# Recurrent layer of a two-layer trunk: gelu of the gate branch as one ScalarE function read from PSUM, and the square of the decay and the first tap of the convolution moved from VectorE to ScalarE

## The reference, cut to what matters

```python
def rglru(x, h0, ga_w, ga_b, gx_w, gx_b, lam):
    r = jax.nn.sigmoid(block_diag(x, ga_w, ga_b).astype(jnp.float32))
    i = jax.nn.sigmoid(block_diag(x, gx_w, gx_b).astype(jnp.float32))
    log_a = -RG_C * r * jax.nn.softplus(-lam.astype(jnp.float32))
    a = jnp.exp(log_a)
    mult = jnp.sqrt(-jnp.expm1(2.0 * log_a))
    bterm = mult * (i * x.astype(jnp.float32))
...
def rglru_mixer(x, conv_buf, h0, w_in, conv_w, conv_b, ga_w, ga_b, gx_w, gx_b, lam, w_out):
    gx = jnp.einsum('bsd,de->bse', x, w_in)
    gate, xr = jnp.split(gx, 2, axis=-1)
    xc, new_buf = causal_dwconv(xr, conv_buf, conv_w)
    xc = xc + conv_b
    h, h_last = rglru(xc, h0, ga_w, ga_b, gx_w, gx_b, lam)
    y = jnp.einsum('bsc,cd->bsd', jax.nn.gelu(gate, approximate=True) * h, w_out)
```

## Time and profile before

| | |
|---|---|
| median of 3 runs | 1391.53 us (1390.49 to 1392.58) |
| span of the profiled execution | 1387.8 us |
| PE, PEld busy | 96%, 64% of the span |
| DVE, ACT, POOL busy | 543.0, 217.6, 122.2 us |
| recurrent mixer on PE | from 704.7 us to about 887 us |
| mean granted TensorE clock | 0.997 of full speed |

### The profile page before, as it was taken

How to read it: one execution, slowest core, us unless ns; L and a number is a source line. 1 busy time by engine, 2 the same in 40 slices (tenths; PEclk the granted TensorE clock), 3 DMA queues, 4 the chain that set the end, 5 groups by cost and what they waited for, 6 DMA issues and landing times.

```text
span 1387.8 us, 20245 instructions
## 1 busy us (share of the span) xinstructions
PE 1337.2 (96%) x8652; PEld 891.7 (64%) x8652; DVE 543.0 (39%) x1157; ACT 217.6 (16%) x383; POOL 122.2 (9%) x138
## 2 busy tenths in 40 slices
PE   8999999999999999998899999999999999999896
PEld 7888875656555555664488888666555555556552
DVE  5677766331111211241446878642211111223217
ACT  0000114000000000100134453310000001010012
POOL 0000001111000110121010000010001100111100
PEclk9999999999999999999999999999999999999999
DMA  9700469999999999999992113899999999999995
GB/s 390 296 5 1 172 278 356 407 426 425 426 427 426 427 424 427 424 425 425 373 327 100 61 61 122 303 380 428 424 427 427 424 427 425 426 426 424 425 404 218
DMA packets 67874, 472.48 MB, mean 340 GB/s; under 512 B 16414, under 2 KB 26654, under 8 KB 40127
## 3 DMA queue, kind: packets, MB, share of 16 engines
q1 hardware_dynamic: 51773, 449.37, 78.1%
q0 software_dynamic: 11520, 15.52, 3.2%
q10 hardware_dynamic: 4490, 6.27, 1.5%
HBM read 468.38 MB, written 27.32 MB: 357 GB/s over the span
## 4 chain that ended last, share of the span: by engine, by line
PE 85%; DMA 10%; ACT 2%; DVE 2%; issue 1%; POOL 0%; POOLq 0%; SPq 0%; DVEq 0%
PE ps L1086 28%; PE ps L1122 14%; PE ps L778 10%; PE ps L732 9%; PE ps L822 7%; PE ps L1051 7%; DMA ring<-in_moe_w_down 3%; DMA ring<-in_moe_w_up 3%; PE ps L1039 3%; PE ps L1110 1%; PE ps L1062 1%; PE ps L839 1%; DMA ring<-yrows 1%; DMA yrows<-A,Bt 1%; PE ps L1224 1%
## 5 line engine op out<-in xcount | busy, mean ns | idle before, releaser
L1086 PE MATMUL ps<-ring,A 128*64 128x256 f32 x4096 | 457.7, 380 | 14.5 <-DMA ring<-in_moe_w_up 6.5
L1086 PEld LDWEIGHTS ps<-ring,A 128*64 128x64 f32 x4096 | 327.4, 137 | 155.1 <-issue 40.0
L1122 PE MATMUL ps<-ring,A 128*64 128x512 f32 x1024 | 233.8, 597 | 7.0 <-issue 1.1
L2026 DVE TENSOR_TENSOR A<-A,ps 128x256 f32<-128x256 f32 x64 | 27.0, 421 | 540.5 <-PE ps L1086 540.5
L1122 PEld LDWEIGHTS ps<-ring,A 128*64 128x64 f32 x1024 | 75.9, 136 | 119.4 <-issue 113.5
L732 PE MATMUL ps<-A,ring 128*128 128x260 f32 x576 | 129.4, 386 | 0.9 <-DMA ring<-in_a_w_in 0.9
L732 PEld LDWEIGHTS ps<-A,ring 128*128 128x128 f32 x576 | 110.5, 192 | 18.5 <-DMA ring<-in_a_w_in 1.2
L667 POOL DMA_INDIRECT A<-x,idx x42 | 44.5, 1060 | 671.9 <-PE ps L1039 623.9
L1051 PE MATMUL ps<-C,Bt 104*64 104x512 f32 x400 | 95.6, 620 | 0.0
L2029 DVE COPY A<-ps 128x256 f32<-128x256 f32 x64 | 27.2, 425 | 121.0 <-PE ps L1110 121.0
L1439 ACT ACTIVATE A<-ps 128x512 f32<-128x512 f32 x42 | 25.1, 598 | 306.1 <-PE ps L1122 306.1
(11 more groups left out here) (295 smaller groups left out, 1137.3 us busy)
## 6 DMA issues: line engine op xcount, KB each, us to landing
ring<-in_moe_w_gate SPq DMA_DIRECT2D x62, 2048.0 KB, 20.3
ring<-in_moe_w_up SPq DMA_DIRECT2D x60, 2048.0 KB, 23.2
ring<-in_moe_w_down SPq DMA_DIRECT2D x60, 2048.0 KB, 29.1
ring<-yrows SPq DMA_DIRECT2D x10, 1024.0 KB, 9.6
ring<-in_a_w_in SPq DMA_DIRECT2D x6, 1536.0 KB
ring<-in_moe_w_down SPq DMA_DIRECT2D x8, 1024.0 KB, 44.1
ring<-in_b_w_in SPq DMA_DIRECT2D x8, 1024.0 KB, 12.0
ring<-in_moe_w_up SPq DMA_DIRECT2D x6, 1024.0 KB, 43.6
```

Of the source, the lines that this page charges most:

```text
L1086: mm = pe.matmul(ps[hf * ROWS:(hf + 1) * ROWS, (GATE_BANK, 3)[u], :FH], xgT[:, k, :], ring[:, slot, col:col + FH], start=(k == 0), stop=(k ...
L1122: mm = pe.matmul(ps[nh * ROWS:(nh + 1) * ROWS, 2, :], hidT[:, at:at + ROWS], ring[:, slot, m * D + nh * 512:m * D + (nh + 1) * 512], start ...
L2026: tt(gated, gated, ps[:, 3, :FH], ALU.mult).then_inc(ready, 1)
```

## The change

The Tanh approximation of the gelu was built of a Copy and a Tanh on ACT and four DVE operations. Now the copy of banks 2 and 3 on ACT is itself the function `Gelu_apprx_tanh`, and `gate_cube`, the Tanh of line 1314 and the DVE operation of line 1735 are gone. The square of the decay moves from DVE (1732) to ACT as `Square`, behind the second Tanh and ahead of the Sqrt. The first tap of the convolution, with its bias, moves from DVE (`tsc` on line 1509, called in `conv`) to ACT as an `Identity` with scale and bias, right behind the copy to `pad`. DVE's last product of a chunk loses its factor 0.5.

```diff
                     act.wait_ge(lam_ok, 3)
                     for c in range(KT):
...
                         act.activation(pad[:, WB - 1:].rearrange("p (a b) -> p a b", a=2), banks(0),
                                        ACT.Copy).then_inc(ev_a[1], 1)
+                        act.wait_ge(ev_a[1], c + 1)
+                        act.activation(tmp[8][:, :SEQ], pad[:, :SEQ], ACT.Identity, bias=feat[:, c, R_BB:R_BB + 1],
+                                       scale=feat[:, c, R_WB:R_WB + 1]).then_inc(tap_in, 1)
                         act.wait_ge(mm_in[1], 2 * c + 2)
                         if c >= 2:
                             act.wait_ge(h_done[1], c - 1)
-                        act.activation(halves(tmp[c % 2]), banks(1), ACT.Copy).then_inc(ev_b[1], 1)
+                        act.activation(halves(tmp[c % 2]), banks(1), ACT.Gelu_apprx_tanh).then_inc(ev_b[1], 1)
                         if c >= 1:
                             recurrence_gates(c - 1)
-                    gelu(KT - 1)
                     early_copies(0, 4)
                     recurrence_gates(KT - 1)
@@ recurrence_gates
-                        if c < KT - 1:
-                            gelu(c)
+                        act.wait_ge(act_gate, 4 * c + 2)
+                        act.activation(tmp[2], tmp[4], ACT.Square).then_inc(act_gate, 1)
                         act.wait_ge(sq_in, c + 1)
-                        act.activation(tmp[2], tmp[2], ACT.Sqrt, scale=0.25).then_inc(act_gate, 1)
+                        act.activation(tmp[2], tmp[2], ACT.Sqrt, scale=-0.25).then_inc(act_gate, 1)
@@ conv, on DVE
-                        step(tsc(G1[:, :SEQ], pad[:, :SEQ], tap(R_WB, c), ALU.mult, tap(R_BB, c), ALU.add))
+                        dve.wait_ge(tap_in, c + 1)
@@ recurrence, on DVE
-                        if c < KT - 1:
-                            gate_cube(c)
                         dve.wait_ge(sig_ok, 2 * c + 2)
                         step(stt(I, I, 1.0, x, ALU.add, ALU.mult))
-                        if c == KT - 2:
-                            gate_cube(KT - 1)
-
-                        dve.wait_ge(act_gate, 4 * c + (2 if c < KT - 1 else 3))
-                        step(stt(R, DEC_A, -1.0, DEC_A, ALU.mult, ALU.mult))
-                        stt(R, R, -1.0, TH, ALU.add, ALU.mult).then_inc(sq_in, 1)
                         dve.wait_ge(act_gate, 4 * c + 3)
-                        step(stt(G, G, 1.0, g, ALU.add, ALU.mult))
+                        stt(R, R, 1.0, TH, ALU.add, ALU.mult).then_inc(sq_in, 1)
...
-                        stt(hT[:, c, :], G, 0.5, TH, ALU.mult, ALU.mult).then_inc(h_done[1], 1)
+                        dve.wait_ge(ev_b[1], c + 1)
+                        tt(hT[:, c, :], g, TH, ALU.mult).then_inc(h_done[1], 1)
```

More of the change, by code:

```diff
@@ L26 @@
 RG_C = 8.0
-GELU_C = 0.7978845608028654
-GELU_A = 0.044715
 GROUPS = 4
@@ L243, in build @@
         pad = C[:, 9 * T:10 * T + WB - 1]
-        def g1_tile(c):
-            return tmp[8] if c < KT - 1 else pad[:, :T]
         xk = [C[:TT, i * D:(i + 1) * D] for i in range(NT)]
@@ L388, in build @@
         act_gate = sem("act_gate")
-        gelu_in = sem("gelu_in")
+        tap_in = sem("tap_in")
         piece_ok = sem("piece_ok")
@@ L1311, in _ @@
                 if l == 1:
-                    def gelu(c):
-                        act.wait_ge(gelu_in, c + 1)
-                        act.activation(g1_tile(c), g1_tile(c), ACT.Tanh, scale=GELU_C).then_inc(act_gate, 1)
                     def recurrence_gates(c):
@@ L1691, in _ @@
                 if l == 1:
-                    R, I, DEC_A, TH, G1 = tmp[2], tmp[3], tmp[4], tmp[5], tmp[8]
+                    R, I, DEC_A, TH, FIRST_TAP = tmp[2], tmp[3], tmp[4], tmp[5], tmp[8]
                     dve.wait_ge(xn_done, 2 * NT)
@@ L1699, in conv @@
                         x = tmp[6 + c % 2]
-                        dve.wait_ge(ev_a[1], c + 1)
+                        out = FIRST_TAP
                         if c >= 2:
                             dve.wait_ge(h_done[1], c - 1)
+                        dve.wait_ge(ev_a[1], c + 1)
                         dve.tensor_copy(new_cols[:, c, :11], pad[:, SEQ:SEQ + 11])
-                        step(tsc(G1[:, :SEQ], pad[:, :SEQ], tap(R_WB, c), ALU.mult, tap(R_BB, c), ALU.add))
-                        step(stt(G1[:, :SEQ], pad[:, 1:SEQ + 1], tap(R_WB + 1, c), G1[:, :SEQ], ALU.mult, ALU.add))
@@ L1706, in conv @@
-                        dve.tensor_copy(G1[:, SEQ:], conv0[:, 1, c, :])
-                        step(stt(G1[:, :SEQ], pad[:, 2:SEQ + 2], tap(R_WB + 2, c), G1[:, :SEQ], ALU.mult, ALU.add))
-                        stt(x, pad[:, WB - 1:], tap(R_WB + 3, c), G1, ALU.mult, ALU.add).then_inc(xc_done, 1)
-                        dve.wait_ge(xc_done, c + 1)
[L1711 to L1718, removed]
+                        dve.tensor_copy(out[:, SEQ:], conv0[:, 1, c, :])
@@ L1720, in recurrence @@
+                        dve.wait_ge(tap_in, c + 1)
+                        step(stt(out[:, :SEQ], pad[:, 1:SEQ + 1], tap(R_WB + 1, c), out[:, :SEQ], ALU.mult, ALU.add))
+                        step(stt(out[:, :SEQ], pad[:, 2:SEQ + 2], tap(R_WB + 2, c), out[:, :SEQ], ALU.mult, ALU.add))
+                        stt(x, pad[:, WB - 1:], tap(R_WB + 3, c), out, ALU.mult, ALU.add).then_inc(xc_done, 1)
+                        dve.wait_ge(xc_done, c + 1)
                     def recurrence(c):
-                        x, g, G = tmp[6 + c % 2], tmp[c % 2], g1_tile(c)
+                        x, g = tmp[6 + c % 2], tmp[c % 2]
```

## The result

| | before | changed |
|---|---|---|
| median of 12 runs each | 1389.7 us | 1392.55 us |
| lowest and highest | 1387.92, 1392.58 us | 1390.15, 1396.64 us |
| span of the profiled execution | 1387.8 us | 1391.3 us |
| DVE, ACT busy | 543.0, 217.6 us | 513.6, 234.4 us |

The ratio is 1.0021 with a 95% interval of 1.0012 to 1.0031: 2.9 us more, from 1.7 to 4.3. This is small, but it stands clear of no difference. The 12 runs of the kernel before that stand beside the changed one have a lower median than the three that the prediction had, by 1.8 us.

A forecast was written before the change was run, and what follows sets the result against it. PE was taken to bound the mixer. Chunk 7's delay, 0.03 + 1.28 + 0.65 - 0.27 = 1.69 us, less 0.21 of room leaves 1.48; 1391.5 + 1.5 = 1393.0 us, range 1390.9 to 1394.6.

The forecast's parts named there:

- The bound, and the cover of DVE's work: In the mixer PE is full, 148.00 of 148.00 us, so taking under 34 us off DVE counts as nothing.
- The middle, cost nothing: In each mid-mixer chunk ACT's Sqrt ends about 0.67 us later, covered by PE's product, so the cost is nothing.
- were ACT over 8.8 us later in each chunk, PE would stop: Claimed limit of ACT's room in the middle of the mixer, 8.8 us in each chunk.
- rival 3: Slower, PE stopping mid-mixer: 1.0 us past ACT's 8.8 us room gives 1397.5 and more, 1399.0 with the end; 3%.
- The end: At the mixer's end a load behind ACT's wait and the Square delay chunk 7's Sqrt 1.69 us, router weights 1.48.
- the two stops: PE idles about 0.4 us near 849.7 at the late products, and 1 us more before the router's first matmuls.
- What becomes of it: Behind the mixer the 1.48 us delay stays in full, with no DMA backlog to absorb it.
- The whole tail moves as one piece: Behind the mixer, experts limited by transfers that begin only then shift by the whole 1.48 us.
- A rule of the Trainium skill: By its 1380 ns drain per switch, chunk 7's new load would cost about 2.66 us, not 1.30; total about 1394.4.
- The sum: Whole kernel: 1.5 us added, span 1387.8 to 1389.3 and median 1391.5 to 1393.0.
- The 3.7 us that I put between span and time: Whole kernel: the median before, 1391.5, was taken to stand 3.7 us above the profiled span of 1387.8.
- the line between no difference and slower: Whole kernel: under 0.2%, 2.8 us, counts as no difference, chance 91%; slower 6%, faster 3%.

The follow-up runs named there:

- runs with a busier middle: Changed kernel with extra table loads and one-column activations on ACT in chunks 0 to 5, 6.1 or 9.1 us a chunk; path 1.87 or 20.1 us longer.
- copies in the chain: Kernel before with seven one-column Copy activations between chunk 7's two Tanh and its Exp; ratio 1.0016, +2.2 us, path +1.40.
- two more loads: Changed kernel with a one-column Sqrt between chunk 7's Tanh and Exp, so two more table loads; ratio 1.0031, +4.3 us against the kernel before.
- load and router weights early: Changed kernel with the Tanh set loaded ahead of the wait for chunk 6 and router weights scaled earlier on DVE; ratio 0.9996 against the kernel before.
- second series: Changed kernel timed again without edit against the kernel before; ratio 1.0021 (1.0009 to 1.0033), path +1.34 us.
- shift without idle time: Kernel before with six spare 128-column matmuls on PE at the start of the recurrent mixer; ratio 1.0007, +1.0 us, path +1.33.

## Why the prediction was right, and where it wasn't

*The bound, and the cover of DVE's work.* Right. PE was full in the middle with 30 us less on DVE (29.4 measured), and nothing came of it.

*The middle, cost nothing.* Right: chunks of 15.78 us, and a Sqrt 0.66 us later (788.68 - 0.36 against 787.66) where 0.67 was worked out. The third load ahead of the gelu started 0.97 us after the tap, at the wait for `h_done`, in ACT's free time. The step "were ACT over 8.8 us later in each chunk, PE would stop" was wrong in its size, and with it the threshold of rival 3: room of one pass was taken for room in every pass. The price of rival 3, 6 us for each microsecond beyond, is what the runs with a busier middle showed, from 5.8 us on and not from 8.8. The change uses about 2 us of either, so the forecast didn't hang on it. One row was misread: the two Tanh from PSUM have a fixed scale of 0.5 and only the bias from memory, so their 0.69 us were no price for both. Nothing in the sum used it.

*The end.* Right, term by term. The load behind the wait was 1.28, the Square 0.64 (0.62 taken), the Sqrt no longer waits for DVE, and it comes 1.64 us later (1.69). Of the two stops the first lost 0.38 us from start to start (0.4 forecast; the profile counts 0.22 of it as idle) and the second was 0.93 (1). PE's path grew by 1.33 and 1.34 us where the sum had 1.48. Of the difference, 0.05 is the Sqrt, and 0.07 is a step that the prediction didn't have: DVE's product with the root starts 0.67 us behind the Sqrt's start (846.72 - 846.05) where it was 0.74 (844.80 - 844.06), as DVE no longer has line 1735 to do just ahead of it. Taking the load out of the chain takes the delay away (+0.10), and a bare delay brings it back (+1.40).

*What becomes of it.* "The whole tail moves as one piece" fits: with a path of +4.14 us the time rose by 4.3 (2.5 to 6.3), which leaves room for a part to be absorbed. The DMA engines had their pause ahead of the next loads in the changed kernel as well, with a share of 0.07 from 904 to 906 us.

*A rule of the Trainium skill.* From load to activation is 1.29 to 1.30 us in the changed kernel wherever the activation had nothing else to wait for (839.93 to 841.23), and no gap of 1380 ns follows. The two loads that were put into the chain moved the Sqrt by 2.80 us together with one small activation of 0.20. This decides against the 2.66 us per switch that the Trainium skill gives ("ScalarE: Activation LUTs", "What ACT_TABLE_LOAD costs"), for loads that stand between activations which depend on each other anyway. The Trainium skill's advice to batch by set ("ScalarE: Activation LUTs", "Table sets: the hidden batching unit") points at the right thing, but what counted was not the number of loads (seven more); it was the one that a wait stood ahead of.

*The sum.* The change was +1.5 us by the forecast and +2.9 (1.7 to 4.3) by the timings, twice. The path explains 1.3 of it, so the forecast of the change is about half of what was measured, below the first interval and just inside the second. That the median came out at 1392.55 with 1393.0 forecast was luck in good part, because two errors cancelled: the three runs shown were 1.8 us above the later median of the kernel before, and the change was put 1.4 us too low. The 3.7 us that I put between span and time are 1.7 for the execution with both on record (1393.04 and 1391.3); by that, the span of 1387.8 us belongs to an execution of about 1389.5 (an estimate), faster than all three. At +0.21% the difference sits on the line between no difference and slower that the chances were given by.

*What stays open.* The 1.6 us above the path. The two intervals leave 0.4 us of it at least in the first series and nothing in the second. No other kernel here shows it: the copies in the chain have 0.8 us above their path and two more loads 0.2, both within the intervals, and 1.6 us would be within them too. The kernel with load and router weights early, which has all of the moved work, leaves 0.7 us at most. So the work on ACT alone doesn't bring the surplus; whether the delay in this chain does is not settled. That the clock makes it was not shown. The fall near 1362 costs 1.5 us where it comes (8.19, 8.19 and 8.14 us instead of 6.67, in both traces of the changed kernel and in the one with load and router weights early), but this last kernel is as fast as the one before, and the copies had no such fall. Nor does the clock of whole executions account for it: in the second series the six executions of the changed kernel with a mean clock of 0.997 or more have a median of 1392.3 us, and the ten such ones of the kernel before in the same series have 1389.5; in the first series the four such ones of the changed kernel have 1390.3. The shift without idle time didn't separate the rest. No version here is faster than the kernel before; the best, with load and router weights early, equals it.

## What to carry to other kernels

Read which engine is full before counting what an edit takes off another; 30 us off an engine that waits were worth nothing. When a function moves an engine between table sets, look for the one place where its load comes to stand behind a wait at the head of a dependent chain; a one-column activation ahead of the wait takes it out. Room that a pass has once is not room in each pass: for that, add up the waits of one pass on the engine that gets the work (5.6 us on ACT here, 5.8 measured). And where a tight chain closes the loop, what an engine is behind by then comes out in full.

## What the runs showed of the hardware that was not expected

`Gelu_apprx_tanh` read 128x520 from PSUM in 0.60 us, as long as a Copy, and a Tanh behind it needed no load. The idle time that the profile gives for a short stop of PE is less than what the stop costs: 0.22 us idle against 0.38 from start to start. The clock was at its lower level for a few us near 1362 in three of the traces. In others, such as that of the kernel before, it was so ahead of the mixer, at a time when PE waited for weights: the windows from 640 to 680 us have 0.96 there. And it was so in the middle of the mixer with 9.1 us more on ACT, behind waits of 3.07 us.

```profile
640.00:680.00 40.00, 33.62 (x232) 19.64 (x230) 5.30 (x10) 3.83 (x7) 1.97 (x2) 0.96 0.93 387
```
